# Attention weights transposed in 32x32 blocks on VectorE, value products on TensorE as 32x64 tiles, in a one-core decoder layer

## The chip, the cores and the metric

The kernel runs on one core of a Trainium2 chip. The metric is the device time of one execution in microseconds (us), the median of several runs. The core has a matrix engine (TensorE, PE in the profile, with its weight loads as a row of their own, PEld), VectorE (DVE), ScalarE (ACT), GpSimd (POOL) and SyncE (SP, which only issues DMAs). Each engine runs its own instruction stream in order; they meet through semaphores.

## The reference

One layer of a decoder for 512 tokens of width 1024, in float32. A combined input projection feeds three mixers in parallel: an RWKV-7 recurrence, a sparse attention (NSA: a compressed, a selected and a sliding branch) and a sliding-window attention with sinks (SWA). Their outputs are projected, gated by sigmoids of the same input, merged, projected and added; then comes a dense SwiGLU FFN. What this change touches is the attention itself, for 8 heads of 64 channels in 2 key groups of 4 heads:

```
s = einsum(q_blk, keys) + rel_bias        # 128 queries x 128..512 keys, per head
p = exp(s - max) / sum                    # masked softmax
o = gate * einsum(p, values)              # 128 queries x 64 channels, per head
```

## The kernel before

The work is cut into 36 *steps* (`STEPS`): for each block i of 128 queries one compressed step (`cmp`), then the NSA steps of two branches b (selected and sliding), then at the end 8 SWA steps. A step has one or two heads of each of the two groups g: two where a head has 128 or 256 keys (i = 0 and 1, and all SWA steps), one where it has 384 or 512 (i = 2, 3). So there are 4 NSA steps each at i = 0 and 1, and 8 each at i = 2 and 3.

For step n the chain is: `qk(n)` on TensorE (scores into two PSUM banks, `R[0:2]`), `scores(n)` on VectorE (adds the bias, takes the minimum, writes `EB`), `exps(n)` on ScalarE, `weights(n)` on VectorE (reciprocals), `weigh(n)` on GpSimd (scales by them), `p_transpose(n)` on TensorE (128x128 transposes of the weights against the identity, into `R[2]` and `R[3]`), `first_half(n)` on VectorE and `second_half(n)` on ScalarE (copies of these banks to `PTB`), and `pv(n)` on TensorE (value products, weights 128 keys x 64 channels, 128 queries streamed). `group_out(o)` copies a finished block of queries from PSUM on ScalarE. All of these are issued by hand-written loops over n, so each engine's order is fixed: TensorE does `qk(n)`, then `fill`, then `p_transpose(n-2)`, then `pv(n-3)`.

`fill(point)` puts dense projection work (the gate columns, 128x128 weights, 512 tokens streamed) between the steps, by the hand-written list `FILL`: two chunks of three products at each step, six matmuls of 512 columns. Other dense work stands before, between and behind. VectorE's `evacs`, GpSimd's `split_upto` (the low parts of weights, which a dense product of three terms needs) and SyncE's weight loads follow the same list. The dense products are fp32r; the transposes and value products are plain fp32, which TensorE runs as two records (a low and a high part of the weights) for each product, and one for each transpose.

`ATT_JOB` is the dense job in work when the attention begins. Just ahead of the attention ScalarE copies the transposed values into `VT`, then splits keys and queries (`KHI`, `QHI`); VectorE makes `KLO`, `QLO`, `KCT` and the compressed values, whose `kv_ok` the first `qk` waits for.

Of the kernel before, what the change touches and what calls it, by code (L numbers as in the profile page):

```python
# [31 lines left out]
HD, NH = 64, 8  # L32
# [245 lines left out]
LAST_CMP = max(n for n in range(NST) if STEPS[n][0] == "cmp")  # L278
PT_ATT = len(FILL); FILL += [2] * (NST + 3)
# [12 lines left out]
ATT_JOB = NS0 + int(np.sum(_ends - 8 < FILLED[PT_ATT - 1] + 8))  # L292
assert all(j[3] == 8 for j in JOBS[NS0:MERGE0])
# [18 lines left out]
def build(nc, x, w_in, w_branch, w_out, w_gate, w_up, w_down, w2, a2, g2, ck1, ck2, cv1, cv2, sinks, rel_bias,  # L312
# [65 lines left out]
    YHI = at("YHI", 90, [P, 4, T], F32R)  # L378
# [3 lines left out]
    VHI = at("VHI", 90, [P, 4, T], F32R)  # L382
# [38 lines left out]
    VCZ = at("VCZ", 108.5, [P, 4, 2, C])  # L421
# [77 lines left out]
    DB4 = [DB[0], DB[1], R[0], R[1]]  # L499

# [47 lines left out]
    def split_of(n):  # L548
# [36 lines left out]
    qk_mm, sc_ok, p_exp, rd_ok, p_ok, snk_ok, p_T, pt_dve, pt_act, pv_mm, o_ev = (sem(s) for s in (  # L585
        "qk_mm", "sc_ok", "p_exp", "rd_ok", "p_ok", "snk_ok", "p_T", "pt_dve", "pt_act", "pv_mm", "o_ev"))
# [86 lines left out]
    with block:  # L673
        @block.sync
        def _(sp):
# [5 lines left out]
            for n in range(FF0):  # L681
# [13 lines left out]
                if n == ATT_JOB + 3:  # L695
                    sp.wait_ge(gn_ok, 4)
                    spilled_before(sp, SW0 + 6)
                    sp.dma_start(SWQ[:, :, :], spilled[0:6].rearrange("b p t -> p b t")).then_inc(swq_in, 16)
                for d in range(GS, KC):
# [65 lines left out]
        def _(pool):  # L765
# [50 lines left out]
            pool.memset(VCZ[:, :, :, :], 0.0).then_inc(zero_ok, 1)  # L816
# [4 lines left out]
            def weigh(n):  # L821
# [8 lines left out]
                for g in range(2):  # L830
                    for jj in range(len(j)):
                        u = len(j) * g + jj
                        at0 = head_cols(n, jj, kind == "swa").start
                        e, rd = EB[:, n % 3, g, at0:at0 + keys_of(n)], STAT[:, n % 4, 2, u:u + 1]
# [7 lines left out]
            for n in range(NST + 3):  # L842
                if n < NST and STEPS[n][0] == "swa":
                    pool.wait_ge(p_T, n - 2)
# [28 lines left out]
        def _(act):  # L873
# [203 lines left out]
            def second_half(n):  # L1077
                act.wait_ge(p_T, n + 1)
                if n >= 2:
                    act.wait_ge(pv_mm, n - 1)  # L1080
# [1875 lines left out]
```

## Time and profile before

| | |
|---|---|
| median of 3 runs | 1002.2 us (1001.81 to 1002.37) |
| span of the profiled execution | 999.8 us; no time of its own is given beside it, so the 2.4 us from the span to the median stand for what lies around a span |
| TensorE busy | 983.0 us, 98% |
| VectorE, ScalarE, GpSimd busy | 692.9, 425.5, 452.3 us |
| attention stretch | 376.6 to 526.0 us, 149.4 us |
| TensorE's granted clock | full in all 40 slices |

A busy TensorE row counts an instruction from its start to its modelled end, and matmuls overlap in it: a 512-column matmul shows about 390 ns, while the next one starts some 230 ns later. What a matmul costs is read from the distance of the starts. "issue" as the end of an idle stretch means that nothing which the profile shows was waited for.

### The profile page before, as it was taken

What the parts mean: (1) busy time and instruction counts of PE and PEld (TensorE: products, weight loads), DVE (VectorE), ACT (ScalarE), POOL (GpSimd) and SP (SyncE); (2) the same over time, 40 slices, a digit from 0 to 9 for tenths busy, and PEclk for the clock granted to TensorE, in tenths of its full rate; (3) what the DMA queues carried; (4) which work ended last, traced back from release to release, by engine and by line L of the source; (5) the groups of instructions that cost most, each with busy time, mean ns of one, the idle gap of its engine ahead of it and who ended that gap; (6) DMA issues with size and microseconds to landing.
All of it is one profiled execution on the core that took longest, in us unless ns stands there. A gap on an engine that the chain in (4) does not pass through costs nothing.

```text
span 999.8 us, 19627 instructions
## 1 busy us (share of the span) xinstructions
PE 983.0 (98%) x7920; PEld 799.7 (80%) x7920; DVE 692.9 (69%) x1160; ACT 425.5 (43%) x829; POOL 452.3 (45%) x511
## 2 busy tenths in 40 slices
PE   6999999999999999999999999999999999999997
PEld 5787777777777777777778888888889998888886
DVE  3799796565566956546556882269887865489987
ACT  4134432322314334546555444545444443345563
POOL 3366557254334766656683448446222234510000
PEclk9999999999999999999999999999999999999999
DMA  9345533122223564112113636433322333244452
GB/s 262 89 129 151 122 92 68 24 65 65 67 66 98 157 159 137 49 50 56 52 54 122 193 116 229 131 127 106 106 85 86 112 106 109 86 136 170 157 176 99
DMA packets 149459, 111.48 MB, mean 112 GB/s; under 512 B 21190, under 2 KB 132048, under 8 KB 149369
## 3 DMA queue, kind: packets, MB, share of 16 engines
q1 hardware_dynamic: 145644, 104.16, 35.7%
q10 hardware_dynamic: 3692, 6.07, 2.2%
q8 instruction: 63, 1.03, 0.4%
q14 instruction: 28, 0.22, 0.1%
q0 software_dynamic: 32, 0.00, 0.0%
HBM read 99.70 MB, written 10.52 MB: 110 GB/s over the span
## 4 chain that ended last, share of the span: by engine, by line
PE 86%; DVE 10%; issue 1%; DMA 1%; POOL 1%; ACT 1%; SPq 0%; DVEq 0%; ACTq 0%
PE ps L2318 33%; PE ps L2798 5%; PE ps L2797 5%; PE ps L2802 5%; PE ps L2332 4%; PE ps L2438 3%; PE ps L2683 3%; PE ps L2858 2%; PE ps L2860 2%; PE ps L2859 2%; PE ps L2625 2%; PE ps L2835 2%; PE ps L2832 2%; PE ps L2831 2%; DVE XF L1430 2%
## 5 line engine op out<-in xcount | busy, mean ns | idle before, releaser
L2318 PE MATMUL ps<-HLO,WHI 128*128 128x512 f32 x440 | 178.2, 405 | 0.4 <-issue 0.4
L2318 PE MATMUL ps<-HHI,WHI 128*128 128x512 f32 x440 | 175.5, 399 | 1.0 <-DVE HLO L1462 0.7
L773 POOL TENSOR_TENSOR WLO<-WRAW,WHI 128x1024 fp32r<-128x1024 f32 (+1 forms) x52 | 104.2, 2006 | 106.5 <-ACT WHI L888 106.5
L869 POOL TENSOR_TENSOR WLO<-WRAW,WHI 128x512 fp32r<-128x512 f32 x50 | 72.3, 1453 | 118.8 <-ACT WHI L1230 117.5
L2318 PE MATMUL ps<-HHI,WLO 128*128 128x512 f32 x440 | 118.1, 398 | 0.0
L777 POOL CAST WHI<-WRAW 128x256 fp32r<-128x256 f32 (+1 forms) x133 | 62.7, 472 | 106.5 <-PE ps L2318 106.3
L808 POOL TENSOR_TENSOR WLO<-WRAW,WHI 128x256 fp32r<-128x256 f32 x132 | 105.6, 800 | 10.7
L2318 PEld LDWEIGHTS ps<-HHI,WHI 128*128 128x128 f32 x440 | 82.6, 188 | 23.2 <-issue 4.7
L2318 PEld LDWEIGHTS ps<-HLO,WHI 128*128 128x128 f32 x440 | 82.6, 188 | 22.7 <-issue 5.1
L2318 PEld LDWEIGHTS ps<-HHI,WLO 128*128 128x128 f32 x440 | 80.5, 188 | 18.3 <-issue 1.4
L2798 PE MATMUL ps<-HLO,WHI 128*128 128x512 f32 x200 | 77.9, 389 | 0.0
L2797 PE MATMUL ps<-HHI,WHI 128*128 128x512 f32 x200 | 77.9, 389 | 0.0
L888 ACT ACTIVATE WHI<-WRAW 128x1024 fp32r<-128x1024 f32 (+1 forms) x51 | 43.5, 854 | 71.7 <-PE ps L2318 67.3
L1073 ACT ACTIVATE EB<-EB,STAT 128x257 f32<-128x257 f32 (+5 forms) x96 | 50.4, 526 | 49.5 <-DVE STAT L1809 42.3
L1230 ACT ACTIVATE WHI<-WRAW 128x512 fp32r<-128x512 f32 x69 | 43.0, 629 | 65.7 <-PE ps L2802 42.1
L2802 PE MATMUL ps<-HHI,WLO 128*128 128x512 f32 x200 | 53.5, 389 | 0.0
L837 POOL TENSOR_SCALAR EB<-EB,STAT,GLT 128x128 f32<-128x128 f32 (+3 forms) x64 | 38.6, 615 | 29.2 <-DVE STAT L1825 29.1
L2802 PEld LDWEIGHTS ps<-HHI,WLO 128*128 128x128 f32 x200 | 37.5, 188 | 7.8
L2797 PEld LDWEIGHTS ps<-HHI,WHI 128*128 128x128 f32 x200 | 37.6, 188 | 7.7
L2798 PEld LDWEIGHTS ps<-HLO,WHI 128*128 128x128 f32 x200 | 37.6, 188 | 7.7
L1832 DVE COPY PTB<-ps 128x512 f32<-128x512 f32 (+3 forms) x36 | 20.6, 572 | 32.2 <-PE ps L2332 32.2
L1809 DVE CUSTOM_DVE_ANT_0 EB<-ps,TB 128x128 f32<-128x128 f32 (+3 forms) x64 | 28.2, 488 | 19.2 <-PE ps L2625 16.9
(517 smaller groups left out, 2404.1 us busy)
## 6 DMA issues: line engine op xcount, KB each, us to landing
WRAW<-in_w_in SPq DMA_DIRECT2D x47, 512.0 KB, 4.4
WRAW<-in_w_gate SPq DMA_DIRECT2D x22, 512.0 KB, 3.8
WRAW<-in_w_up SPq DMA_DIRECT2D x22, 512.0 KB, 3.9
WRAW<-in_w_down SPq DMA_DIRECT2D x19, 512.0 KB, 3.4
spilled<-SQ SPq DMA_DIRECT2D x24, 256.0 KB, 2.4
GATES<-spilled SPq DMA_DIRECT2D x6, 768.0 KB, 4.8
WRAW<-in_w_in SPq DMA_DIRECT2D x16, 256.0 KB, 3.7
WRAW<-in_w_branch SPq DMA_DIRECT2D x32, 128.0 KB, 2.9
```

What stands on the lines that cost most here:

```text
L773: return pool.tensor_tensor(lo[:, 0:chunks, :], WRAW[:, n % NRAW, 0:chunks, :], hi[:, 0:chunks, :].bitcast(F32), ALU.subtract)
L777: return pool.tensor_copy(WHI[:, slot_of(n), k0:k1, :], WRAW[:, n % NRAW, k0:k1, :])
L808: lo = pool.tensor_tensor(WLO[:, slot_of(n), k:k + 2, :], WRAW[:, n % NRAW, k:k + 2, :], WHI[:, slot_of(n), k:k + 2, :].bitcast(F32), ALU. ...
L869: pool.tensor_tensor(lo, raw_half(item[1], item[2]), hi.bitcast(F32), ALU.subtract).then_inc(w_lo, 1)
L888: act.activation(split_of(n)[0][:, 0:width_of(n), :], WRAW[:, n % NRAW, 0:width_of(n), :], ACT.Copy).then_inc(w_hi, 1)
L1073: last = act.activation(EB[:, n % 3, g, cols], EB[:, n % 3, g, cols], ACT.Exp, scale=-1.0, bias=st[:, 0, u:u + 1], accum_out=st[:, 1, u:u ...
L1230: act.activation(item_slot(m)[0], raw, ACT.Copy).then_inc(w_hi, 1)
L2318: last = pe.matmul(DB[g % 2][:, :], (wlo if which == "low" else whi)[:, c, :], lo if which == "x_low" else hi, start=a == 0, stop=a == 3 * ...
L2332: return pe.transpose(dst, src, ident[0:n, 0:n])
L2797: pe.matmul(dst, hi[:, kk, :], HHI[:, k, :], start=k == 0, stop=False)
L2798: pe.matmul(dst, hi[:, kk, :], HLO[:, k, :], start=False, stop=False)
L2802: last = pe.matmul(dst, lo[:, kk, :], HHI[:, k, :], start=False, stop=k == 7)
```

## The change

The weights of attention are no longer transposed on TensorE. VectorE's `turned(n)` transposes them in place in `EB`, each block of 32 queries x 32 keys for itself. So the keys of a block of 128 now lie on partitions in four groups of 32 (a): group a holds the weights of queries 32a to 32a+31, for keys 32r to 32r+31 in the columns of block r. For this the values stand in `V4` (`SV4` for SWA) once for each group of 32 partitions, brought there by 16 DMAs each: for i = 0 from ScalarE's queue (`v4_first`), for i = 1 to 3 from SyncE's at `ATT_JOB + 1` (`v4_rest`), and for SWA from SyncE's at `SINK_JOB` (`sv4_in`). A value product is a tile of 32 keys x 64 channels with 64 columns streamed (32 queries of two heads). There are 8 such tiles, 4 groups of partitions and 2 key groups, and a loop over (k, r, a, g) goes round them. Two heads are handled in one *event*: where a step has one head, the event waits for two steps. `EB` has 6 buffers instead of 3. The results of partition group a go to bank `R[2 + a]`, and `group_out` makes four copies of a quarter instead of one. `first_half`, `second_half`, `p_transpose` and `PTB` are gone.

```diff
-    STEPS += [("nsa", _i, tuple(range(_j, _j + _nj)), _b) for _j in range(0, 4, _nj) for _b in range(2)]
+    for _pair in range(0, 4, 2):
+        STEPS += [("nsa", _i, tuple(range(_j, _j + _nj)), _b) for _b in range(2) for _j in range(_pair, _pair + 2, _nj)]
...
+                if n == ATT_JOB + 1:
+                    sp.wait_ge(vtok_ok, 2)
+                    for a in range(4):
+                        for b in range(4):
+                            sp.dma_start(V4[rows32(a), b, :, 1:4, :], VST[rows32(b), :, 1:4, :]).then_inc(v4_rest, 16)
...
-                act.activation(VT[:, b, :, :], R[2 + b][:, :].rearrange("p (a b) -> p a b", a=4),
+                act.activation(VST[:, b, :, :], R[2 + b][:, :].rearrange("p (a b) -> p a b", a=4),
                                ACT.Copy).then_inc(vtok_ok, 1)
-
+            act.wait_ge(vtok_ok, 2)
+            for a in range(4):
+                for b in range(4):
+                    act.dma_start(V4[rows32(a), b, :, 0, :], VST[rows32(b), :, 0, :]).then_inc(v4_first, 16)
...
-            def first_half(n):
-                dve.wait_ge(p_T, n + 1)
-                if n >= 2:
-                    dve.wait_ge(pv_mm, n - 1)
-                w = keys_of(n) * max(1, len(STEPS[n][2]))
-                dve.tensor_copy(PTB[:, n % 2, 0, 0:w], R[2][:, 0:w]).then_inc(pt_dve, 1)
+            def turned(n):
+
+                dve.wait_ge(p_ok, n + 1)
...
+                w = keys_of(n) + (STEPS[n][0] == "swa")
+                p = EB[:, SLOT[n], :, 0:w * len(STEPS[n][2])].rearrange("p g (j c) -> p g j c", c=w)[:, :, :, 0:keys_of(n)]
+                dve.transpose(p, p).then_inc(pt_ok, 1)
...
+                for k in range(kb):
+                    t = i + 1 - kb + k
+                    for r in range(4):
+                        at0 = P * k + 32 * r
+                        for a in range(4):
                             for g in range(2):
-                                last = pe.matmul(bank[half[g], j[jj] * P:(j[jj] + 1) * P], VT[:, b, i + 1 - kb + k, half[g]],
-                                                 PTB[:, n % 2, g, to + k * P:to + (k + 1) * P],
-                                                 start=opens and jj == 0 and k == 0, stop=k == kb - 1, skip_group_check=True)
+                                values = V4[rows32(a), r, b, t, half[g]] if kind == "nsa" else SV4[rows32(a), t // 2, r, t % 2, half[g]]
...
+                                last = pe.matmul(R[2 + a][half[g], cols], values, p, start=opens and k == 0 and r == 0,
+                                                 stop=k == kb - 1 and r == 3, skip_group_check=True)
```

On TensorE, in an NSA step of i = 3 (512 keys), the rows before are these (L2625 is `qk`, L2318 the fill, L2332 the transposes, L2683 the value products; a count is one of products, of which an fp32 one has two records):

```order
L2625 MATMUL ps<-KHI_110,QHI 128x512
L2625 MATMUL ps<-KLO_112,QHI 128x512 x2
L2625 MATMUL ps<-KHI_110,QLO 128x512 x2
L2318 MATMUL ps<-HHI,WLO 128x512 x3
L2318 MATMUL ps<-HHI,WHI 128x512 [waits dense_evac,w_hi]
L2318 MATMUL ps<-HLO,WHI 128x512
L2318 MATMUL ps<-HHI,WHI 128x512
L2332 MATMUL ps<-CONP,EB 128x128 [waits pt_act,pt_dve,p_ok]
L2332 MATMUL ps<-CONP,EB 128x128 x7
L2683 MATMUL ps<-PTB,VT 64x128 [waits pt_act,pt_dve]
L2683 MATMUL ps<-PTB,VT 64x128 x7
```

And these are the rows of the change for the same block of queries, where an event follows two steps (L2670 is `qk`, L2362 the fill, L2723 the value products):

```order
L2670 MATMUL ps<-KHI_112,QHI 128x512
L2670 MATMUL ps<-KLO_114,QHI 128x512 x2
L2670 MATMUL ps<-KHI_112,QLO 128x512 x2
L2362 MATMUL ps<-HHI,WLO 128x512 x3
L2362 MATMUL ps<-HHI,WHI 128x512 [waits dense_evac,w_hi]
L2362 MATMUL ps<-HLO,WHI 128x512
L2362 MATMUL ps<-HHI,WHI 128x512
L2723 MATMUL ps<-EB,V_102 64x64 [waits pt_ok]
L2723 MATMUL ps<-EB,V_102 64x64 x127
```

The 8 transposes and 8 value products of each step have become 128 value products once in two steps, with nothing between them. In the whole program 224 transposes and 216 value products of NSA and SWA steps go and 1728 value products come; the `cmp` steps keep 8 value products each, now of 32 keys.

On ScalarE, just ahead of the attention, the rows of the change are these; before, the DMA rows are not there and `VT` stands for `VST`:

```order
L1076 ACTIVATE VST<-ps 128x512
L1081 DMA V_102<-VST 32x2x128 [waits vtok_ok]
L1081 DMA V_102<-VST 32x2x128 x15
L1084 ACTIVATE KHI_112<-NQ 128x512
L1084 ACTIVATE KHI_113<-NQ 128x512
L1087 ACTIVATE QHI<-NQ 128x4x128 x3
```

The splits of keys and queries have moved behind 16 DMA issues.

## Rows read from the trace of the kernel before

**Rows 1.** The page: busy times, TensorE's clock in 40 slices, the instruction queue

```profile
PE 983.0 (98%) x7920; PEld 799.7 (80%) x7920; DVE 692.9 (69%) x1160; ACT 425.5 (43%) x829; POOL 452.3 (45%) x511
...
PEclk9999999999999999999999999999999999999999
...
q8 instruction: 63, 1.03, 0.4%
```

**Rows 2.** Busy time by engine over the attention stretch

```profile
376.60:526.00 149.40, 149.13 (x1273) 115.67 (x1274) 82.33 (x313) 76.36 (x243) 101.87 (x188) 1.00 0.23 65
```

**Rows 3.** The group of TensorE's value products, by line and shape: busy, mean

```profile
L2683 PE MATMUL ps<-PTB,VT 128*64 128x128 f32 x432 | 30.6, 280 | 0.0
```

**Rows 4.** Timeline of TensorE, a step of 512 keys: start, length, count

```profile
480.22 0.50 PE L2318 MATMUL ps<-HLO,WHI 128*128 128x512 f32 x1
480.56 1.32 PE L2318 MATMUL ps<-HHI,WLO 128*128 128x512 f32 x5
481.71 1.03 PE L2332 MATMUL ps<-CONP,EB 128*128 128x128 f32 x8
482.68 1.09 PE L2683 MATMUL ps<-PTB,VT 128*64 128x128 f32 x16
483.70 0.49 PE L2630 MATMUL ps<-SWQ 64*128 64x128 f32 x4
```

**Rows 5.** Timeline of TensorE in the RWKV stretch: 64x64 tiles, four at once

```profile
217.41 0.69 PE L2438 MATMUL ps<-XX,AM 64*64 64x64 f32 x32
217.93 0.65 PE L2438 MATMUL ps<-AM,XX 64*64 64x64 f32 x32
```

**Rows 6.** Timeline of TensorE in the same stretch, between two idle moments

```profile
176.44 0.39 PE L2318 MATMUL ps<-HLO,WHI 128*128 128x512 f32 x1 [0.38 <-issue]
...
177.91 0.69 PE L2438 MATMUL ps<-XX,UI 64*64 64x64 f32 x32
178.43 0.65 PE L2438 MATMUL ps<-NW 64*64 64x64 f32 x32
179.01 0.50 PE L2318 MATMUL ps<-HLO,WHI 128*128 128x512 f32 x1
179.34 0.62 PE L2318 MATMUL ps<-HHI,WLO 128*128 128x512 f32 x2
179.95 1.04 PE L2438 MATMUL ps<-NW 64*64 64x64 f32 x54
181.36 0.39 PE L2438 MATMUL ps<-NW 64*64 64x64 f32 x10 [0.37 <-issue]
```

**Rows 7.** A third such moment, TensorE's timeline at 214.7 to 216.6 us

```profile
214.73 1.04 PE L2438 MATMUL ps<-NW 64*64 64x64 f32 x54
216.14 0.44 PE L2438 MATMUL ps<-NW 64*64 64x64 f32 x10 [0.37 <-issue]
```

**Rows 8.** DMA in 178.65 to 179.95, 180 to 181.36, 182.65 to 184.3 us

```profile
q8 instruction: 1, 0.02, 5.9%
...
DMA packets 0, 0.00 MB, mean 0 GB/s; under 512 B 0, under 2 KB 0, under 8 KB 0
...
DMA packets 2, 0.02 MB, mean 15 GB/s; under 512 B 0, under 2 KB 0, under 8 KB 0
```

**Rows 9.** DMA issues on ScalarE's and SyncE's queues, and what follows ScalarE's values

```profile
362.32 0.37 ACTq L1034 DMA_DIRECT2D TBS<-bias_rows  x1
367.29 1.15 ACT L1044 ACTIVATE KHI<-NQ 128x512 fp32r<-128x512 f32 x2
...
372.09 0.93 SPq L711 DMA_DIRECT2D WRAW<-in_w_in  x1
```

**Rows 10.** Timelines of VectorE and TensorE where the attention begins

```profile
373.88 1.16 DVE L1754 COPY VCZ<-ps 31x128 f32<-31x128 f32 x4
...
376.61 1.06 PE L2636 MATMUL ps<-KCT,NQ 64*128 64x7 f32 x16
```

**Rows 11.** The page: VectorE's copies of transposed weights

```profile
L1832 DVE COPY PTB<-ps 128x512 f32<-128x512 f32 (+3 forms) x36 | 20.6, 572 | 32.2 <-PE ps L2332 32.2
```

More of the change, by code:

```diff
@@ L278 @@
 LAST_CMP = max(n for n in range(NST) if STEPS[n][0] == "cmp")
+EVENTS = []
+for _n in range(NST):
+    _kind, _i, _j, _b = STEPS[_n]
+    if len(_j) == 1 and _j[0] % 2:
+        EVENTS[-1] += (_n,)
+    else:
+        EVENTS.append((_n,))
+EVENT_OF = {_n: _e for _e, _steps in enumerate(EVENTS) for _n in _steps}
+EVENT_AT = {_steps[-1]: _e for _e, _steps in enumerate(EVENTS)}
+SCORED = [n for n in range(NST) if STEPS[n][0] != "cmp"]
+NEB = 6
+SLOT = {n: m % NEB for m, n in enumerate(SCORED)}
+HELD = {n: SCORED[m - NEB] for m, n in enumerate(SCORED) if m >= NEB}
+HALF_DONE = max(n for n in range(NSA_STEPS) if STEPS[n][2] and STEPS[n][2][0] < 2)
 PT_ATT = len(FILL); FILL += [2] * (NST + 3)
@@ L292 @@
 ATT_JOB = NS0 + int(np.sum(_ends - 8 < FILLED[PT_ATT - 1] + 8))
+SINK_JOB = NS0 + int(np.sum(_ends <= FILLED[PT_ATT + HALF_DONE + 1] + 8)) + NRAW
 assert all(j[3] == 8 for j in JOBS[NS0:MERGE0])
@@ L499, in build, with rows32 @@
     DB4 = [DB[0], DB[1], R[0], R[1]]
+    def rows32(a):
+        return slice(32 * a, 32 * a + 32)
     def head_cols(n, jj, sink=0):
@@ L1744, in queries_low @@
                 dve.wait_ge(split_hi, 10 + i)
-                dve.tensor_tensor(QLO[:, :, tokens], NQ[:, 0:4, tokens], QHI[:, :, tokens].bitcast(F32),
+                part = slice((i - 1) * P, i * P)
+                dve.tensor_tensor(QLO[:, :, part], NQ[:, 0:4, tokens], QHI[:, :, part].bitcast(F32),
                                   ALU.subtract).then_inc(split_lo, 1)
@@ L1752, in _ @@
             dve.wait_ge(zero_ok, 1)
-            for j in range(4):
-                ins = dve.tensor_copy(VCZ[32 * j:32 * j + NCMP, j, :, :],
+            for a in range(4):
+                ins = dve.tensor_copy(VC4[32 * a:32 * a + NCMP, :, :],
                                       R[1][0:NCMP, 128:256].rearrange("p (a b) -> p a b", a=2))
@@ L1782, in scores @@
                 dve.wait_ge(qk_mm, n + 1)
-                if n >= 3:
-                    dve.wait_ge(p_T, n - 2)
+                if n in HELD:
+                    dve.wait_ge(pv_mm, EVENT_OF[HELD[n]] + 1)
+                if kind != "cmp" and SLOT[n] == NEB - 1 and n not in HELD:
+                    dve.wait_ge(v4_first, 256)
+                    dve.wait_ge(v4_rest, 256)
                 if kind == "cmp":
@@ L2619, in qk @@
                     k = (KHI[2 * b], KLO[2 * b]) if kind == "nsa" else (WKHI, WKLO)
+                    part = slice((i - 1) * P, i * P) if kind == "nsa" else tokens
                     pe.wait_ge(split_lo, 18 + i if kind == "nsa" else 22 + i)
@@ L2624, in qk @@
                             for g in range(2):
-                                last = pe.matmul(R[g][:, head_cols(n, jj)], q[a][half[g], j[jj], tokens], k[b_][half[g], keys],
+                                last = pe.matmul(R[g][:, head_cols(n, jj)], q[a][half[g], j[jj], part], k[b_][half[g], keys],
                                                  start=a + b_ == 0, stop=a == 1)
@@ L2670, in pv @@
                 if kind == "cmp":
[L2671 removed]
+                    for a in range(4):
                         for g in range(2):
[L2673 to L2685 removed]
+                            last = pe.matmul(R[2 + a][half[g], 0:P], VC4[rows32(a), g, :], ECBT[rows32(a), g, :, :],
+                                             start=True, stop=False, skip_group_check=True)
@@ L2691, in _ @@
                 fill(PT_ATT + n)
[L2692 to L2695 removed]
+                if n - 3 in EVENT_AT:
+                    pv(EVENT_AT[n - 3])
             for i in range(4):
```

140 lines of the change are left out of this document (68 added, 72 removed).

## The prediction

> **What bounds the kernel now.** I read the page first. TensorE is busy for 98% of the span, at full clock throughout, while VectorE, ScalarE and GpSimd are at 69, 43 and 45% [rows 1]. Then the stretch of the attention: TensorE is busy for 149.1 of 149.4 us, GpSimd for 101.9, VectorE for 82.3, ScalarE for 76.4 [rows 2]. So TensorE sets the pace there, and what it saves or loses there comes out at the end, since it is as full behind it. What TensorE pays for a form is read from the distance of starts in its timeline, as busy time counts overlapping records.
>
> **What a product costs now.** In a step of 512 keys, 8 transposes take 0.97 us to the first value product, 8 value products (16 records) take 1.02 us to the next `qk` [rows 4]. I take 0.1 and 0.15 us of these for the change of shape, and so 0.109 us for each. A `cmp` step has 2 transposes and 8 products, 1.35 us by the same. The dense products stand 0.23 us apart; a fill of six with its entry is 1.49 us, from 480.22 to 481.71 [rows 4]. The value products of NSA and SWA are 432 records for 216 products [rows 3].
>
> **What a small tile costs.** No row has tiles of 32x64. The nearest are the 64x64 tiles of the RWKV stretch, four at once: 16 products (32 records) of 64 columns in 0.52 us, 32.5 ns each [rows 5]. Some 0.05 us of that is the entry, in which nothing overlaps yet, so I take 0.47 us, 29.2 ns each. With eight tiles in place of four it is half, 14.6 ns. Bounds: not less than 14.6, since each tile still needs its own time, and not more than 29.2, if only four run at once. I take 14.6, because the eight tiles have their own partitions and banks as the four have.
>
> **The work on TensorE, part by part.**
> - NSA, 512 keys: each pair of steps has 2 x 1.99 us now, and in its place 128 x 14.6 ns + 0.15 = 2.02. Saved 1.96, four times: 7.8.
> - 384 keys: 2 x (6 + 6) x 0.109 + 4 entries = 3.10 against 96 x 14.6 ns + 0.15 = 1.55; four times: 6.2.
> - 256 keys, two heads (4 NSA and 6 SWA steps): 1.99 against 64 x 14.6 ns + 0.15 = 1.08; ten times: 9.1.
> - 128 keys (4 and 2): 1.13 against 0.62; six times: 3.1.
> - `cmp`: 2 transposes and 8 products, 1.35, against 8 products on eight tiles, 0.38; four times: 3.9.
>
> Together 30.1 us less: the stretch would take 119.3 us.
>
> **What feeds TensorE.** Here the change costs what it saves. It has 2 x 1728 records of products, each with a weight load, where it had 432 + 216 and their loads: 6912 instructions against 1296, and they come in bursts of up to 512 at 3.65 ns apiece. Queue q8 brings 63 packets of 1.03 MB together, 16 KB each; TensorE's 15,840 records [rows 1] are 251 for each packet. So a packet is a chunk of TensorE's instructions, some 256. Now the idle moments that nothing explains. At 181.36 TensorE goes on after 0.37 us, 54 products into a batch of 64 that has no wait inside; at 176.44 it had done so as well. Between them stand six dense products, 32, 32, 1, 2 and 54: 127, with their loads 254 instructions, one chunk [rows 6] (five single rows like the first are left out there). At 216.14 it is again after 54 of 64 [rows 7]. In the DMA view one packet of q8 lies in 178.65 to 179.95 (5.9% of 16 engines over 1.30 us: 1.23 us), and none from there to 181.36; the next is in 182.65 to 184.3 [rows 8]. So a chunk is asked for once the one before it is entered, the transfer begins 1.3 us (181.36 to 182.65) to 2.2 us (176.44 to 178.65) after that, lasts 1.0 (0.4% of 16 x 999.8 us over 63 packets [rows 1]) to 1.2 us, and its instructions run 1.4 us or more after its end. Together 3.7 to 4.9 us for 256 instructions; I take 4.1, that is 16 ns for each instruction. Now the attention's 2547 records [rows 2] are 10 chunks, 15 us each, and the supply is never felt.
>
> **The Trainium skill on this.** "Runtime: NRT & Kernel Launch", section on instruction fetch mechanics, says that TensorE holds 2048 instructions, refilled in blocks of 256, and that crossing a block is mostly hidden. By that rule the bursts would run at full rate. The trace disagrees: with 2048 held, the moments at 181.36 and 216.14 would not be there, 0.37 us each.
>
> **The sum of the stalls.** For each burst I set the instructions from its start to the next one's, at 16 ns, against TensorE's own time for them. `qk` I estimate at 0.95 us for 512 keys (three passes at the 0.23 us of a dense product, both key groups at once, and 0.25 for the shapes), at 0.8 and 0.9 for 384 and for two heads of 256.
> - 512 keys: 564 instructions, 9.0 us, against 6.9 (two `qk`, two fills, 2.02), three times; the fourth has one short step behind it, 8.8 against 4.4. Excess 10.7.
> - 384 keys: 7.0 against 6.1 three times, 6.6 against 4.0 once: 5.3.
> - 256 keys, NSA: 4.6 against 3.5, four times: 4.4.
> - SWA of 256 keys: 4.7 against 3.5 twice; the last have no `qk`, 4.3 against 2.6 three times, and about 1 at the end: 8.5.
> - 128 keys and `cmp`: 170 instructions are 2.7 us against 3.1; nothing.
>
> That is 28.9 us. The chunks do not fall evenly: one that lies whole in a burst needs 0.9 us of work and 4.1 of supply, and a slow one beside it gives nothing back except what TensorE's queue holds. Priced chunk by chunk this is up to 7 us more; I add 3.
>
> **The start.** ScalarE issues 16 DMAs between the copies of the values and `KHI`. One issue took 0.37 us; the longest on SyncE in that stretch took 0.93 [rows 9]. 16 are 5.9 us (up to 15). Behind them on ScalarE are `KHI` and `QHI`; for `KHI` waits VectorE, in order, and behind that wait are a dense evacuation, `QLO`, and the copies after which `qk` begins. The copies ended at 375.04, `qk` began at 376.61 [rows 10]. `KHI` slips from 367.3 to 373.3, `kv_ok` to about 378, `scores(0)` by 2.4. So 2.4 us (0 if the issue is quicker and the fill covers it, 11 at 0.93 each). SyncE's two lots of 16 stand ahead of weight loads that are four jobs ahead of use; at 5.9 us each these are hidden, and `v4_rest` is not needed before the sixth score step, five steps of some 4 us on.
>
> **The other engines.** VectorE loses 36 copies, 20.6 us [rows 11], of 14,336 columns (one of the two key groups), 1.44 ns a column, and gets transposes of twice as many, 28,672: 41.2 us at that price, 0 at the least. So it goes from 82.3 to at most 102.9 us of a stretch of 150, hidden by TensorE's own pace and by its stalls; without that cover it would be the 20.6 us. ScalarE loses its copies and gets 24 quarter copies, less than it loses. One `EB` buffer is freed by a value product six steps later, never late. `group_out` now stands between a group's last product and the next group's first, with a `qk` and a fill (2.3 us) to hide it. For such waits I add 1.0.
>
> **Sum.** -30.1 + 28.9 + 3.0 + 2.4 + 1.0 = +5.2 us on 149.4, so a span of 1005.0, and with the 2.4 us that the median has over the span 1007.4 us.
>
> **The rivals.**
> - *The supply keeps up* (the other side). Place: the chunks of the attention. If the fetch is as fast as the bursts, or more is held than one chunk, the stalls go: -30.1 + 2.4 + 1.0, 975.5 us. For it: only three such moments were seen, all of 0.37 us. Against it: at 4.92 us for a chunk the supply was already the limit. The bursts and what follows them are some 6500 instructions, 25 chunks, so 0.1 us on a chunk is 2.5 us: it decides at 3.9 us for a chunk, where the sum is nothing. Chance 0.15 for a supply that is not felt; one at 3.7 us counts with the forecast.
> - *Four tiles at once.* 1728 x 29.2 ns adds 25 us of work, but bursts at half the rate outrun the supply less: of 29 + 3 us of stalls some 12 remain. -4.9 + 12 + 3.4: 1012.7 us. Chance 0.12.
> - *A floor for each matmul.* Were no start closer than 25 ns to the last, 3456 records took 86.4 us instead of 25.2, with no stalls left: -30.1 + 61.2 + 3.4, 1036.7 us. Four tiles show 32 records in 0.52 us, 16 ns [rows 5], so this has a chance of 0.03. That floor stands in the Trainium skill, "TensorE: Matmul & The Clock Gate", section on 56 against 53.3 ns; by that rule the trace disagrees.
> - *The clock falls* in stalls of up to 3 us. Clock 1.00 stands in every slice, the first with TensorE's wait for its data among them [rows 1], so no row prices the lower level; if a quarter of the 90 us from the first burst of 256 on ran at 1.2 GHz, at twice its length, it would be 22 us more, 1029. Chance 0.05.
>
> **How the numbers follow.** What a measurement of this kernel can tell from no change is about 0.2%, 2 us. The forecast has 0.65. A supply of 3.7 us makes it 997.4, one of 4.9 makes it 1027.4, the start's 0 to 11 us add -2.4 to +8.6; its own range is 996 to 1022, with 0.09 of its chance faster, 0.10 the same and 0.46 slower. Faster: 0.15 + 0.09 = 0.24. Same: 0.10. Slower: 0.46 + 0.12 + 0.03 + 0.05 = 0.66. A range that leaves out the fast rival, the floor and the worst of the clock is 990 to 1024.
>
> **What would show it.** TensorE idle for 1 to 3 us at a time inside L2723, released by nothing ("issue"), one chunk of 256 apart; some 32 packets of q8 in the attention instead of 10; 85 in all. Eight starts of L2723 within 58 ns where it does not stall. TensorE's first `qk` about 2 us later after ScalarE's values than before, behind 16 ACTq rows. Wrong would be: no such idle moments, or bursts at twice the pitch.

## The result: 2.3% slower

The changed kernel takes 1025.4 us in the median of 4 runs (1021.6 to 1026.6), the kernel before 1002.0 (1001.7 to 1002.4): a ratio of 1.023, with a 95% interval of 1.021 to 1.024. The forecast was 1007.4 with a range of 990 to 1024, so the direction was right and the size was not: 23.4 us more than before where 5.2 were forecast. The profiled execution took 1026.4 us, its span is 1024.6, 24.8 us over that of the profile before.

First the page of the profile after, with the lines that answer to [rows 1], [rows 3] and [rows 11]: one form of the value products and VectorE's transposes, each with busy time and mean, then the idle time before it:

```profile
PE 985.6 (96%) x10720; PEld 797.8 (78%) x10720; DVE 704.2 (69%) x1160; ACT 411.4 (40%) x817; POOL 451.3 (44%) x511
...
PEclk9999999999999998989999999999999999999999
...
q8 instruction: 85, 1.39, 0.6%
...
L2723 PE MATMUL ps<-EB,V 32*64 32x64 f32 x2560 | 33.5, 233 | 11.1 <-issue 11.0
...
L1876 DVE STREAM_TRANSPOSE EB<-EB 128x1024 f32<-128x1024 f32 (+2 forms) x32 | 33.8, 1056 | 1.4 <-POOL EB L876 1.4
```

TensorE is as long busy as before, and idle for 39 us instead of 17. The instruction queue brought 85 packets, as forecast (63 before). What is new is that the clock is no longer full in all slices.

Then the attention stretch, from its first `qk` to the end of the last value product, in one window, and pieces of it (us, busy by engine, granted clock, DMA share, GB/s), which answers to [rows 2]:

```profile
382.87:551.62 168.75, 151.40 (x4086) 113.56 (x4086) 95.96 (x315) 61.99 (x228) 101.69 (x188) 0.92 0.29 80
...
376.00:383.00 7.00, 0.83 (x6) 0.37 (x4) 3.77 (x11) 3.99 (x6) 0.00 (x0) 0.78 0.21 67
383.00:390.00 7.00, 7.00 (x33) 5.52 (x34) 3.97 (x19) 0.89 (x4) 1.12 (x2) 0.50 0.62 153
...
440.00:460.00 20.00, 18.39 (x475) 13.92 (x475) 9.76 (x28) 4.34 (x13) 8.83 (x16) 0.83 0.16 43
...
500.00:520.00 20.00, 15.28 (x528) 12.42 (x523) 6.97 (x30) 6.32 (x29) 8.03 (x19) 0.83 0.12 30
```

It begins 6.3 us later than before (382.87 against 376.61 [rows 10]) and lasts 168.8 us against 149.4, which together are 25.6 us; 0.8 of them come back behind it. VectorE has 96.0 us of work in it, less than the 102.9 of the forecast, and is not what it waits for. The granted clock is 0.92 over 168.75 us. Its two levels are 2.4 GHz, which is 1.00, and 1.2 GHz, which is 0.50, so for 16% of the stretch, 27 us, it stood at 1.2 GHz.

What TensorE waited for, in the view of waits from 382 to 552 us (sum, times, longest):

```profile
PE ps L2723 <- issue: 12.7, 9, 2.8
PE ps L2681 <- DVE VC L1789: 6.2, 1, 6.2
PE ps L2670 <- issue: 2.5, 2, 1.8
PE ps L2362 <- POOL WHI L814: 1.3, 3, 0.6
PE ps L2670 <- DVE STAT L1847: 0.5, 1, 0.5
```

The 15.2 us of "issue" (15.4 with the moments too short for this view) are the stall that was forecast, at half its size. 6.2 us is the start. 1.8 us are the other waits.

Now TensorE's timeline. First the undisturbed bursts of 64, 128 and 192 records, with the row behind each, which answers to [rows 4]:

```profile
398.71 0.91 PE L2723 MATMUL ps<-EB,V 32*64 32x64 f32 x64
399.56 0.62 PE L2681 MATMUL ps<-KCT,NQ 64*128 64x15 f32 x8
...
415.35 1.59 PE L2723 MATMUL ps<-EB,V 32*64 32x64 f32 x128
416.88 1.07 PE L2681 MATMUL ps<-KCT,NQ 64*128 64x23 f32 x16
...
449.43 2.27 PE L2723 MATMUL ps<-EB,V 32*64 32x64 f32 x192
451.63 0.45 PE L2670 MATMUL ps<-KHI,QHI 64*128 64x384 f32 x2
```

From start to the next work they take 0.85, 1.53 and 2.20 us. The entry is 0.17 and each further 32 products (64 records) are 0.68 and 0.67 us: 21.1 ns for a product, not 14.6. Then a piece of the sliding windows in which TensorE stands for its instructions, and what follows:

```profile
530.47 0.38 PE L2670 MATMUL ps<-WKHI,WQLO 64*128 64x256 f32 x1 [0.76 <-issue]
...
532.37 1.53 PE L2723 MATMUL ps<-EB,SV 32*64 32x64 f32 x121
534.20 0.34 PE L2723 MATMUL ps<-EB,SV 32*64 32x64 f32 x7 [0.31 <-issue]
...
536.97 1.30 PE L2723 MATMUL ps<-EB,SV 32*64 32x64 f32 x102
539.70 0.47 PE L2723 MATMUL ps<-EB,SV 32*64 32x64 f32 x26 [1.42 <-issue]
...
541.40 0.63 PE L2362 MATMUL ps<-HHI,WHI 128*128 128x512 f32 x1
541.83 0.63 PE L2362 MATMUL ps<-HLO,WHI 128*128 128x512 f32 x1
542.26 0.63 PE L2362 MATMUL ps<-HHI,WHI 128*128 128x512 f32 x1
```

Between the idle moments at 530.47 and 534.20 stand 1 record of `qk`, 6 dense ones and 121 of the burst. These are 128 records, with their loads 256 instructions, in 3.73 us; to 539.70 it is 7 + 12 + 6 + 102 = 127 records, in 5.50. So the chunks are as long as the prediction had them. Behind the idle moment of 1.42 us the dense products start 0.43 us apart, where they stood 0.23 apart before it: TensorE runs at half clock for a while.

The DMA view points to the supply too. Here is a burst of 512 keys, and the view from 513.10 to 514.30 us:

```profile
511.52 2.30 PE L2723 MATMUL ps<-EB,V 32*64 32x64 f32 x196
515.77 0.97 PE L2723 MATMUL ps<-EB,V 32*64 32x64 f32 x60 [1.95 <-issue]
```

```profile
q8 instruction: 1, 0.02, 6.2%
```

The one packet in this window takes 1.19 us of its 1.20 (6.2% of 16 engines), and 1.5 us after its end TensorE goes on. At each of the ten idle moments of 0.3 us and more with "issue" behind them it goes on 1.2 to 1.6 us after the end of a packet of q8, and from one to the next there are whole chunks of 256 (254 to 1272 instructions, each within 8 of a whole number). The stretch of the attention has 31 such packets, where it had 10 and the prediction expected some 32.

The Trainium skill, "Runtime: NRT & Kernel Launch", section on instruction fetch mechanics, has 2048 instructions held and crossing a block mostly hidden. By that rule none of these moments would exist; the trace disagrees, with these ten, 15.1 us in sum.

Last, the start: ScalarE's queue and TensorE, which answer to [rows 9] and [rows 10]:

```profile
367.46 10.98 ACTq L1081 DMA_DIRECT2D V<-VST  x16
378.50 1.15 ACT L1084 ACTIVATE KHI<-NQ 128x512 fp32r<-128x512 f32 x2 [11.06 <-issue]
```

```profile
375.63 1.07 PE L2362 MATMUL ps<-HHI,WLO 128*128 128x512 f32 x4
382.87 1.88 PE L2681 MATMUL ps<-KCT,NQ 64*128 64x7 f32 x16 [6.17 <-DVE VC L1789]
```

The 16 issues took 11.0 us, 0.69 each. `KHI` slipped by 11.2 us, and of that TensorE stood for 6.2.

### The profile page after: what moved, and what is told of

It reads as the page before. It is cut to its first block, busy times and chain, and to the rows that moved or that the text cites. A ratio compares the mean times of both kernels' runs of the same rounds, so it can differ in the third digit from the quotient of the medians.

```text
span 1024.6 us, 25136 instructions
## 1 busy us (share of the span) xinstructions
PE 985.6 (96%) x10720; PEld 797.8 (78%) x10720; DVE 704.2 (69%) x1160; ACT 411.4 (40%) x817; POOL 451.3 (44%) x511
## 4 chain that ended last, share of the span: by engine, by line
PE 83%; DVE 10%; issue 3%; ACTq 1%; POOL 1%; ACT 1%; DMA 1%; DVEq 0%; SPq 0%
PE ps L2362 32%; PE ps L2835 5%; PE ps L2834 5%; PE ps L2839 5%; PE ps L2723 4%; PE ps L2482 3%; PE ps L2895 2%; PE ps L2897 2%; PE ps L2896 2%; PE ps L2670 2%; PE ps L2872 2%; PE ps L2869 2%; PE ps L2868 2%; DVE XF L1464 2%; PE ps L2376 2%
## 5 line engine op out<-in xcount | busy, mean ns | idle before, releaser
L2362 PE MATMUL ps<-HLO,WHI 128*128 128x512 f32 x440 | 181.1, 412 | 0.6 <-issue 0.6
L2362 PE MATMUL ps<-HHI,WHI 128*128 128x512 f32 x440 | 178.4, 405 | 2.0 <-POOL WHI L814 1.3
L2362 PE MATMUL ps<-HHI,WLO 128*128 128x512 f32 x440 | 120.5, 404 | 0.0
L2362 PEld LDWEIGHTS ps<-HHI,WHI 128*128 128x128 f32 x440 | 84.5, 192 | 25.5 <-issue 5.0
L2362 PEld LDWEIGHTS ps<-HLO,WHI 128*128 128x128 f32 x440 | 84.1, 191 | 23.6 <-issue 5.4
L2362 PEld LDWEIGHTS ps<-HHI,WLO 128*128 128x128 f32 x440 | 81.9, 191 | 18.6 <-issue 1.4
L2835 PE MATMUL ps<-HLO,WHI 128*128 128x512 f32 x200 | 77.9, 389 | 0.0
L2834 PE MATMUL ps<-HHI,WHI 128*128 128x512 f32 x200 | 77.9, 389 | 0.0
L1264 ACT ACTIVATE WHI<-WRAW 128x512 fp32r<-128x512 f32 x69 | 43.0, 629 | 65.8 <-PE ps L2839 42.2
L2839 PE MATMUL ps<-HHI,WLO 128*128 128x512 f32 x200 | 53.4, 389 | 0.0
L1847 DVE CUSTOM_DVE_ANT_0 EB<-ps,TB 128x128 f32<-128x128 f32 (+3 forms) x64 | 28.2, 487 | 31.5 <-PE ps L2670 26.8
L2723 PE MATMUL ps<-EB,V 32*64 32x64 f32 x2560 | 33.5, 233 | 11.1 <-issue 11.0
L2723 PEld LDWEIGHTS ps<-EB,V 32*64 32x64 f32 x2560 | 30.1, 131 | 18.0 <-issue 17.9
```

The costliest lines, as they stand in the source:

```text
L1264: act.activation(item_slot(m)[0], raw, ACT.Copy).then_inc(w_hi, 1)
L2362: last = pe.matmul(DB[g % 2][:, :], (wlo if which == "low" else whi)[:, c, :], lo if which == "x_low" else hi, start=a == 0, stop=a == 3 * ...
L2723: last = pe.matmul(R[2 + a][half[g], cols], values, p, start=opens and k == 0 and r == 0, stop=k == kb - 1 and r == 3, skip_group_check=True)
L2834: pe.matmul(dst, hi[:, kk, :], HHI[:, k, :], start=k == 0, stop=False)
L2835: pe.matmul(dst, hi[:, kk, :], HLO[:, k, :], start=False, stop=False)
L2839: last = pe.matmul(dst, lo[:, kk, :], HHI[:, k, :], start=False, stop=k == 7)
```

## The experiments

Twelve kernels ran, each against the kernel before on the same chip. The times are medians of four runs; span and mean granted clock are those of the profiled execution. "Less" and "more" below are against the changed kernel's 1025.4 us, if nothing else is named:

| kernel | us | ratio to before, 95% | span | mean clock |
|---|---|---|---|---|
| `start_sp` | 1014.9 | 1.010 to 1.014 | 1015.3 | 0.989 |
| `half_products` | 986.8 | 0.983 to 0.986 | 983.7 | 0.993 |
| `no_turn` | 1024.0 | 1.020 to 1.023 | 1022.5 | 0.985 |
| `wide` | 1014.9 | 1.011 to 1.014 | 1013.1 | 0.986 |
| `wide_start` | 1007.2 | 1.003 to 1.006 | 1005.1 | 0.990 |
| `wide_all_start` | 982.9 | 0.979 to 0.982 | 982.0 | 0.997 |
| `narrow` | 1031.1 | 1.026 to 1.031 | 1026.2 | 0.978 |
| `spread` | 1019.1 | 1.014 to 1.019 | 1017.0 | 0.991 |
| `issues_alone` | 1010.9 | 1.008 to 1.011 | 1009.0 | 0.994 |
| `quad` | 990.8 | 0.987 to 0.990 | 988.2 | 0.998 |
| `fill_start` | 1019.1 | 1.016 to 1.019 | 1017.0 | 0.990 |
| `quad_free` | 990.5 | 0.986 to 0.990 | 988.4 | 0.997 |

### The start

`start_sp`: the changed kernel with the 16 issues off ScalarE's queue.

```diff
-            act.wait_ge(vtok_ok, 2)
-            for a in range(4):
-                for b in range(4):
-                    act.dma_start(V4[rows32(a), b, :, 0, :], VST[rows32(b), :, 0, :]).then_inc(v4_first, 16)
...
-                            sp.dma_start(V4[rows32(a), b, :, 1:4, :], VST[rows32(b), :, 1:4, :]).then_inc(v4_rest, 16)
+                            sp.dma_start(V4[rows32(a), b, :, :, :], VST[rows32(b), :, :, :]).then_inc(v4_first, 16)
```

Expected: 

> SyncE issues the 16 copies of the values (all four token blocks at once) where it issued v4_rest; ScalarE goes straight on to KHI and QHI. Theory A (the start: 16 issues of 0.69 us ahead of KHI hold TensorE for 6.17 us, and the granted clock of 0.50 behind that idle moment costs another 3 to 4 us): the idle moment at 382.87 goes, the clock stays at 1.00 there, 8 to 10 us less than the changed kernel, about 1016. Theory B (only what TensorE waited, the clock is the chip's own affair): 6 us less, 1019.5, with half clock still in that stretch. My own prediction's term, 2.4 us: 1023.

Measured: 1014.9 us, 10.5 less. The idle moment is gone and the clock from 383 to 390 us is 1.00. That is theory A, with half a microsecond more than it gave.

`issues_alone`: the kernel before with those 16 issues and nothing else.

```diff
+            act.wait_ge(vtok_ok, 2)
+            for a in range(4):
+                for b in range(4):
+                    act.dma_start(V4[32 * a:32 * a + 32, b, :, :], VT[32 * b:32 * b + 32, 0:2, 0, :]).then_inc(v4_first, 16)
```

Expected: 

> The kernel before, with nothing of the change but 16 DMA issues on ScalarE between the copies of the values and KHI; they copy the first block of values to memory that nobody reads. Theory A (the start is a wait of its own, 6.2 us of idle TensorE and half clock for some 10 us behind it, whatever the value products are): 8 to 11 us over the kernel before, 1010 to 1013, with one idle moment of about 6 us before the first scores of the compressed keys and a granted clock near 0.5 in the 7 us behind it. Theory B (my prediction's price, 0.37 us an issue and 2.4 us of TensorE): 1004.5. In both the rest of the attention has no idle moment over 0.5 us.

Measured: 1010.9 us, 8.9 more than before. Its timeline, and the window behind the idle moment:

```profile
382.97 1.88 PE L2644 MATMUL ps<-KCT,NQ 64*128 64x7 f32 x16 [6.44 <-DVE VCZ L1762]
...
386.23 0.63 PE L2326 MATMUL ps<-HHI,WHI 128*128 128x512 f32 x1
386.66 0.63 PE L2326 MATMUL ps<-HLO,WHI 128*128 128x512 f32 x1
```

```profile
383.00:390.00 7.00, 7.00 (x34) 5.53 (x35) 3.98 (x18) 0.79 (x4) 1.12 (x2) 0.54 0.52 141
```

The same idle moment and the same half clock appear with value products as before, and in the rest of the attention there is no idle moment over 0.3 us. So both belong to the start: 6.4 us of idle time, and 3.2 us (46% of 7) lost to the clock behind it. The sum of both is a little more than the 8.9 us measured.

### What a burst costs

`half_products`: two of the four blocks of 32 keys left out in each block of 128.

```diff
-                    for r in range(4):
+                    for r in (0, 3):
```

Expected: 

> Leaves out half of the value products of NSA and SWA (two of the four 32-token rows of each block), 3456 TensorE instructions, 13.5 chunks; the output is not the reference's. Theory A (supply and entry of instructions set the pace in the bursts: the bursts take 46 us in the profile after, with 15.6 us of idle moments marked issue and some 20 us of half clock behind them): half of 46, all of 15.6 and some 8 us for the clock go, 45 us less, about 980, and no idle moment over 0.3 us is left in L2723. Theory B (products cost 14.6 ns each and only the idle moments are the supply's): 12.6 + 15.6, 28 us less, 997. Theory C (VectorE or GpSimd paces the stretch): under 10 us less.

Measured: 986.8 us, 38.6 less, between the two theories (980 and 997) and nearer to A. In L2723 itself no idle moment over 0.3 us is left, as A has it, but one of 2.1 us stands at the `qk` right behind a burst; the other waits are 6.4 us at the start and 3.9 for weights of the dense work:

```profile
PE ps L2681 <- DVE VC L1789: 6.4, 1, 6.4
PE ps L2362 <- POOL WHI L814: 3.9, 5, 1.3
PE ps L2670 <- issue: 2.1, 1, 2.1
```

The run takes away instructions and columns together and does not tell them apart; `narrow` and `wide_all_start` do more for that.

`no_turn`: the transposes of VectorE cut to their first 32 columns.

```diff
-                dve.transpose(p, p).then_inc(pt_ok, 1)
+                dve.transpose(p[:, :, :, 0:32], p[:, :, :, 0:32]).then_inc(pt_ok, 1)
```

Expected: 

> Leaves out all but the first 32 columns of each of VectorE's transposes in NSA and SWA; TensorE's instructions stay the same; the output is not the reference's. Theory A (supply): VectorE is hidden, within 2 us of the changed kernel, with the same idle moments. Theory C (VectorE's transposes are late for the bursts): 5 us or more less, and fewer waits of TensorE in L2723.

Measured: 1024.0 us, 1.4 less, and 15.2 us of "issue" in TensorE's waits as before. So VectorE's transposes are not the cause.

`narrow`: half of the columns of each product, the same instructions.

```diff
-                cols = slice(32 * j[0], 32 * j[0] + 64)
+                cols = slice(32 * j[0], 32 * j[0] + 32)
...
-[:, :, at0:at0 + 32]
+[:, :, at0:at0 + 16]
```

Expected: 

> The changed kernel with 32 columns in each value product where it has 64 (half of the queries are left out, the output is not the reference's); the number and order of TensorE's instructions are the same. Theory A (supply and entry of instructions set the bursts): within 3 us of 1025.4, the same idle moments, the same pitch of 8 to 13 ns per record. Theory B (the columns set the burst's 46 us): 12 us less or more than that.

Measured: 1031.1 us, 5.6 more, with half of the columns gone. Its undisturbed bursts:

```profile
399.07 0.86 PE L2723 MATMUL ps<-EB,V 32*64 32x32 f32 x64
399.86 1.07 PE L2681 MATMUL ps<-KCT,NQ 64*128 64x15 f32 x16
...
447.46 2.11 PE L2723 MATMUL ps<-EB,V 32*64 32x32 f32 x192
449.50 0.44 PE L2670 MATMUL ps<-KHI,QHI 64*128 64x384 f32 x2
```

0.79 and 2.04 us: 1.25 us for 64 products, 19.5 ns each, against 21.1 with twice the columns. So at 64 columns nearly all of a product's price does not depend on its columns. Spread over its two records and two loads it is some 5 ns each; whether it lies in the instructions or in the tile is not told apart, since no run changes the one without the other. That the kernel came out slower was in neither theory; its mean clock is 0.978 against 0.984, which is 6 us of its span.

`wide`: 128 columns, all four heads of a group, in one product where a step has 128 or 256 keys.

```diff
-    if len(_j) == 1 and _j[0] % 2:
+    if _j and _j[0] // len(_j) % 2:
...
-                                    p = EB[rows32(a), SLOT[n], g, 0:2 * w].rearrange("p (j c) -> p j c", c=w)[:, :, at0:at0 + 32]
+                                    p = EB[rows32(a), SLOT[n]:SLOT[n] + 2, g, 0:2 * w].rearrange("p s (j c) -> p s j c", c=w)[:, :, :, at0:at0 + 32]
```

Expected: 

> For 128 and 256 keys and all SWA steps one product takes all four heads, 128 columns in place of two products of 64: 416 of 1728 products go, 1664 instructions, 6.5 chunks, with the columns the same. Theory A1 (what costs is the instruction: supply and entry): 832 records at 8.4 ns are 7.0 us, the idle moments at 421.75, 530.47, 534.20 and 539.70 (3.2 us) and the half clock behind the last (1.7 us) go: 12 us less, 1013.5. Theory A2 (in a burst the columns cost, the instructions only in idle moments): 5 us less, 1020.5.

Measured: 1014.9 us, 10.5 less: nearer to A1 (1013.5) than to A2 (1020.5). q8 has 78 packets, seven fewer for 1664 instructions fewer. The idle moments marked "issue" are gone in the sliding windows; for them one wait of 2.2 us for weights of the dense work has come.

`wide_start`: the edits of `wide` and `start_sp` together.

Expected: 

> Both edits that were 10.5 us each: the copies of the values on SyncE, and 128 columns for four heads where a step has 128 or 256 keys. Theory A (the start is a wait of its own, the wide products save supply elsewhere): the gains add, 1025.4 - 21.0 = 1004.4 us, still not below the kernel before, since the bursts of 384 and 512 keys are left. Theory B (a stall removed in one place comes back in the next chunk): 1008 or more.

Measured: 1007.2 us. The gains add to 18.2 of 21.0 us, between A and B: at the bursts of 384 and 512 keys 12.1 us of "issue" are left, 1.6 more than in `wide`.

`wide_all_start`: `wide_start` with 128 columns for 384 and 512 keys too, with other columns than the reference needs.

```diff
-                    for r in range(4):
+                    for r in range(0, 4, 3 - len(j)):
...
-                                    p = EB[rows32(a), SLOT[n]:SLOT[n] + 2, g, at0:at0 + 32]
+                                    p = EB[rows32(a), SLOT[n]:SLOT[n] + 2, g, at0:at0 + 64]
```

Expected: 

> wide_start, and for 384 and 512 keys one product of 128 columns in place of two of 64 (it takes the queries of the next 32 keys as further columns instead of two more heads, so the output is not the reference's, the columns are the same): 448 products go, 1792 instructions, 7 chunks. Theory A (the instruction is what costs): 896 records at 8.4 ns are 7.5, the idle moments of 384 and 512 keys some 9, the half clock behind them some 5: 21 us under wide_start, about 983. Theory B (columns cost in the burst): 14 us under it, 990. If the supply had nothing to do with it: as wide_start.

Measured: 982.9 us, 24.3 under `wide_start`. It streams the same columns with 1792 instructions fewer, q8 has 71 packets, "issue" falls from 12.1 to 1.2 us, and the mean clock rises from 0.990 to 0.997. This is the clearest of the runs: with the same columns in fewer and wider products, the stalls go and the time with them.

`spread`: six bursts of 384 and 512 keys cut in two.

```diff
+                if n - 4 in EVENT_AT and in_two(EVENT_AT[n - 4]):
+                    pv(EVENT_AT[n - 4], 1)
                 fill(PT_ATT + n)
```

Expected: 

> The six bursts of 384 and 512 keys that are not the last of their group are cut in two, with the next step's scores between the halves; nothing else moves. Theory A (the average supply of 564 instructions for 6.9 to 7.6 us of work sets the stretch): the idle moments are shorter and more, their sum falls by at most 3 us, 1022 to 1025. Theory B (what costs is that a chunk lies whole in a burst, and that idle moments of 2 us take the clock down): 6 us less or more, 1019, with no half clock from 441 to 520.

Measured: 1019.1 us, 6.3 less, as theory B has it. But TensorE's "issue" fell only from 15.2 to 13.0 us, as theory A has it. What moved is the clock: 9.2 us of the span lost to it ((1 - 0.991) x 1017.0), 16.4 in the changed kernel. The idle moments are shorter, and more of the time is at 2.4 GHz. The longest moment that stayed (2.4 us at 485.55) has half clock again: 0.83 in 480 to 500 us. Two of 1.9 us stayed as well; the clock is 0.91 in 500 to 520, where one of them lies, and 1.00 in 520 to 540, where the other does.

`fill_start`: `start_sp` with seven units of three dense products moved from behind the attention to the sliding windows.

```diff
+for _n in (30, 32, 33, 34, 35, 36, 37):
+    FILL[PT_ATT + _n] += 1
...
-PT_TAIL = len(FILL); FILL += [5, 5, 5]
+PT_TAIL = len(FILL); FILL += [4, 3, 3]
```

Expected: 

> start_sp, and seven units of dense products (21 products, 4.9 us) moved from behind the attention into seven steps of the sliding windows, ahead of their bursts; the work is the same. Theory A (TensorE idles there for its instructions, which dense products of 0.23 us a pair of instructions give time to come): the dense work runs in what was idle, 4 to 5 us less than start_sp, 1010.5, and the idle moments of the sliding windows (some 5.8 us in start_sp) shrink to under 2. Theory B (the stretch is full of work): 1015, the idle moments as before and the stretch 4.9 us longer.

Measured: 1019.1 us, 4.2 more than `start_sp`: neither. From 505 us on its waits are

```profile
PE ps L2359 <- POOL WHI L816: 4.1, 2, 2.9
PE ps L2720 <- issue: 2.9, 3, 1.5
PE ps L2359 <- POOL WLO L812: 1.9, 1, 1.9
```

The idle moments of the sliding windows' own bursts shrank as A has it, from 5.8 to 1.4 us (the third of the 2.9 us is the last burst of 512 keys). But the dense products now come before GpSimd has their weights ready, 6.0 us. The time was free on TensorE, not on GpSimd. The two profiled executions lie only 1.7 us apart in span (1017.0 and 1015.3), so these waits explain that much, and the rest of the 4.2 us is open.

### A version that beats both

`quad` is `start_sp` with four heads in one product at all lengths, with room made for eight weight buffers. The core of it:

```diff
-    if len(_j) == 1 and _j[0] % 2:
+    if _j and _j[0]:
...
-NEB = 6
-SLOT = {n: m % NEB for m, n in enumerate(SCORED)}
+NEB = 8
+_slots = [0, 1, 2, 3] * 2 + list(range(8)) * 2 + [0, 1, 2, 3, 4, 5, 0, 1]
+SLOT = dict(zip(SCORED, _slots))
...
-                                    p = EB[rows32(a), SLOT[n]:SLOT[n] + 2, g, at0:at0 + 32]
+                                    p = EB(n)[rows32(a), SLOT[n]:SLOT[n] + 4, g, at0:at0 + 32]
```

Expected: 

> All four heads in one value product of 128 columns at every length: for 384 keys eight weight buffers of 384 columns, for 512 keys eight of 516, of which the last two take the bias rows of heads that are done (bias rows stored in pairs, the sink values moved to memory that is free by then), and the start as in start_sp. 864 of the 1728 products are left, 13.5 chunks fewer than the changed kernel. It computes the reference. Theory A (the instruction supply sets the bursts): as wide_all_start, 983, 19 us below the kernel before. Theory B (a burst now comes once in four steps with all its instructions at once, and its last steps are new waits): idle moments of 2 to 3 us in each burst of 384 and 512 keys, 992 or more.

Measured: 990.8 us, 11.2 us (1.15%) below the kernel before. It lies 7.8 us above `wide_all_start`. Its waits from 365 to 530 us tell part of it:

```profile
PE ps L2373 <- POOL WHI L832: 4.1, 4, 2.2
PE ps L2735 <- issue: 2.9, 5, 1.2
PE ps L2681 <- DVE STAT L1858: 2.6, 5, 1.5
PE ps L2681 <- issue: 1.6, 1, 1.6
PE ps L2681 <- DVE ECB L1851: 1.1, 1, 1.1
```

The wait for `WHI` is no part of it, since `wide_all_start` has 4.4 us of it. But "issue" is 4.5 us here against 1.2 there, and the waits for VectorE are 3.7 against 1.3. A burst of 512 keys is again 256 records at once, and VectorE, with 92.2 us of work in 134.3, is late for some scores: part of theory B. Its bursts with 128 columns:

```profile
391.67 1.21 PE L2735 MATMUL ps<-EB,V 32*64 32x128 f32 x64
392.81 0.39 PE L2681 MATMUL ps<-KHI,QHI 64*128 64x256 f32 x2
...
414.54 2.10 PE L2735 MATMUL ps<-EB,V 32*64 32x128 f32 x128
416.56 0.45 PE L2681 MATMUL ps<-KHI,QHI 64*128 64x384 f32 x2
```

1.14 and 2.02 us, 27.5 ns for a product of 128 columns, where two of 64 are 42.2.

`quad_free`:

```diff
-                        dve.wait_ge(pv_mm, EVENT_OF[n])
+                        dve.wait_ge(pv_mm, EVENT_OF[max(m for m in range(n) if STEPS[m][0] == "cmp")] + 1)
```

Expected: 

> quad with one wait of VectorE moved: its transpose of a compressed step waited for the value products of every step before it, and now waits only for those of the compressed step before, which read the same buffer. In the profile of quad VectorE stood 2.76 us there in the group of 384 keys, and TensorE then waited for its scores at 438.58 (1.08 us), 453.14 (0.48) and 460.66 (1.50). Theory A (these come from that wait): 2 to 3 us less than quad's 990.75, 988. Theory B (VectorE is the bound of these steps by its own work, sink copies of 1.09 us and transposes of 1.22 us in each step): within 1 us of quad.

Measured: 990.5 us, as `quad`. VectorE's wait of 2.8 us is gone from its profile, and TensorE's at 439.41, 453.91 and 461.44 are still there with 1.07, 0.40 and 1.52 us. That is theory B. VectorE works without a break from 449.08 us to the waits at 453.91 and 461.44, so its own work sets those two; at 439.41 it had itself waited 1.2 us for TensorE before the work that TensorE then waits for.

## Why the prediction was wrong, step by step

The table sets the terms of its sum against the two profiles. The work on products is the time from one start to the next on TensorE, summed over the records of these lines, without idle time: transposes 28.2, value products 27.5 and `cmp` products 4.1 before (59.8 us), 44.7 and 2.0 after.

| term | predicted | measured |
|---|---|---|
| transposes and value products | -30.1 | -13.1 |
| supply: idle moments | +28.9 + 3.0 | +15.4 |
| the start: idle time | +2.4 | +6.2 |
| other waits | +1.0 | +1.8 |
| the rest of TensorE's work in the stretch, mostly at half clock | 0 | +15.3 |
| sum | +5.2 | +25.6 |

The first two rows are off by 17.0 us one way and by 16.5 the other and nearly cancel. What carries the forecast of +5.2 to +25.6 is the 15.3 us on the rest of TensorE's work, most of it the clock, for which the sum had nothing, and the start with 3.8 more.

- **What bounds the kernel, and where it would stall: right.** There were 85 packets of q8, chunks of 256 instructions, and ten idle moments of 0.3 to 2.8 us that nothing releases, eight of them inside L2723 and two at the `qk` behind it.
- **"I take 14.6, because the eight tiles have their own partitions and banks as the four have": the step that failed first.** It was the low end of 14.6 to 29.2 ns; a product takes 21.1. The halving from four tiles at once to eight was not there: 16 ns from record to record with 64x64 tiles [rows 5] became 10.6, not the 7.3 of the forecast. `narrow` shows that columns are not the reason, since with half of them a product still takes 19.5. 1728 products at 6.5 ns more are 11.2 of the 17.0 us.
- **The supply: a term that was too big, in part because the one above was too small.** The chunk took 3.73 us at 530.47 and 5.50 before 539.70, around the 4.1 assumed. The bursts, longer by a half, gave it more time to come: by the prediction's own working, 21.1 ns in place of 14.6 takes some 10 of the 28.9 us (the 11.2 without the bursts of 128 keys, which had no stall in the sum). The stretches at half clock gave it more still, and 15.4 us of 31.9 were left. Too little for one term was too much for the other, as the rival of four tiles at once had worked out. That the two errors cancel is luck.
- **The start: mis-sized.** An issue cost 0.69 us, not 0.37; the row taken was a single large DMA on the same queue, and the bound of 0.93 was nearer. The chain (issues, `KHI`, VectorE in order, `qk`) was right, and with 11.0 us of issues in place of 5.9 the prediction's own working gives 7.5, where 6.2 were measured.
- **The clock: the term put at nothing, and the largest part of the miss.** It was a rival with 0.05 that came to pass with the forecast, not in place of it. The full clock "in every slice" of before said nothing of idle moments of 2 us and more, since there were none within the attention. 15.3 us of the 25.6 are the fills (59.6 to 70.3 us) and the `qk`s (29.9 to 34.5) of unchanged work; a mean clock of 0.92 is 13.5 us over the stretch, nearly all of it on this work (in the timeline 1.8 of the 27 us at half clock fall on the bursts), and some 2 us are the last dense product ahead of a burst, which takes 0.32 us to the next start instead of 0.23, 24 times. The rival was priced as if it stood beside the forecast, when each forecast stall was a chance for it.
- **The rivals.** A supply that keeps up (975.5) and four tiles at once (29.2 ns a product) are excluded by the rows above, and so is a floor of 25 ns for each matmul, with 10.6 ns from record to record. The clock rival's 1029 is the nearest number, in part by luck: its 22 us for the clock were some 8.5 too many (13.5 by the mean clock), and the 1007.4 that it was added to was too few by some 4.5 without the clock.
- **VectorE, buffers and SyncE's issues put at nothing: nothing speaks against it.** `no_turn` moves the time by 1.4 us, less than the runs of one kernel lie apart. VectorE's 32 transposes took 33.8 us, between 0 and the 41.2 assumed.

The idle moments do not all bring half clock. In the profile after it follows those of 6.17, 2.17, 1.93, 2.77, 1.95 and 1.42 us and not those of 1.78, 1.26, 0.76, 0.71 and 0.31. Only for the start is it shown by a run with nothing else changed (`issues_alone`) that the wait brings the half clock with it. Idle moments are not the whole of it: in `narrow` the clock is 0.91 from 400 to 420 us, where the changed kernel has 1.00, and no idle moment over 0.2 us stands in that window. What decides is open, and so is why `narrow` lost 6 us more to it than the changed kernel. The time is also less steady: the runs of the changed kernel spread over 5 us, those of before over less than 1. That this is the clock's doing is not shown.

## What to carry to other kernels

Count instructions before columns when tiles get small. Here a product of 32x64 by 64 columns took 21.1 ns, some 5 for each of its four instructions, and where the supply could not keep up a chunk of 256 instructions took 3.73 to 5.50 us, some 15 to 21 ns for each; one product of 128 columns costs 27.5 ns where two of 64 cost 42.2. Look for the widest product that the buffers allow before the work is split. Work with few instructions for its time, put between the bursts, shortened the stalls here (`fill_start`), but it gained nothing, because the engine that feeds it had no room.

Price an idle moment of TensorE at more than its own length: 6.4 us in an otherwise unchanged kernel were followed by a stretch at half clock that cost another 3. A forecast of several stalls needs a term for this, and not a rival beside it, though not each stall brought it.

A row of small DMAs issued from an engine's queue is work of that engine: 16 took 11 us here, and what stood behind them was what TensorE waited for.

## What the hardware did that was not expected

- Sixteen DMAs from memory to memory on the chip, 32 partitions each, cost ScalarE 0.69 us apiece and SyncE 0.65 (10.4 us for 16), while a single large load cost ScalarE 0.37.
- Half clock for some 3 to 10 us at idle moments of 1.42, 1.93, 1.95, 2.17, 2.77 and 6.17 us in a stretch that is otherwise full; none at those of 0.71, 0.76, 1.26 and 1.78 us.
- Halving the columns of 64-column products saved 1.6 ns of 21.1 each.
